# The next norm's sum of squares from block sums and a carried sum, at both junctions of a three-layer f32 kernel

## What is computed

```python
for i in range(2):                              # layers 0 (gated spatial unit) and 1 (latent attention)
    shift, scale, gate = split(silu(c) @ ada_w[i] + ada_b[i])
    h = rms_norm(x, pre_g[i]) * (1 + scale) + shift
    y = mixer_i(h)                              # ends with  ... @ w_out
    x = x + gate * rms_norm(y, post_g[i])
h = rmsnorm(x, norm_mix)                        # layer 2 begins so
z = h @ w_in
```

## Time and profile before

| | |
|---|---|
| median of 3 runs | 2478.34 us (2477.54 to 2480.36) |
| profiled execution | 2477.93 us, span 2476.1 us |
| PE busy | 2433.2 us (98%) |
| DVE busy | 1889.0 us (76%) |
| ACT busy | 1399.4 us (57%) |
| POOL busy | 442.0 us (18%) |

### The profile page before, as it was taken

The page is one execution under the profiler, slowest core; times in us unless marked ns, Lnnn a source line. Parts: engine busy times, 40 slices in busy tenths (PEclk is TensorE's granted clock), DMA queues, the critical chain, the costliest instruction groups (busy, mean ns, idle before and its releaser), DMA issues.

```text
span 2476.1 us, 31108 instructions
## 1 busy us (share of the span) xinstructions
PE 2433.2 (98%) x11597; PEld 2018.7 (82%) x11597; DVE 1889.0 (76%) x2295; ACT 1399.4 (57%) x1934; POOL 442.0 (18%) x298
## 2 busy tenths in 40 slices
PE   6999999999999999998999999999999999999999
PEld 5888888888887989887888888888888888888887
DVE  7899798977777787866655555557988878788884
ACT  6655765444447555555566676755655545555553
POOL 0264563111020000110000000043111021111111
PEclk9999999999999999999999999999999999999999
DMA  9999677978784877754555556455465555646454
GB/s 364 321 341 349 237 256 273 336 283 290 271 313 149 246 212 220 233 208 149 167 173 163 177 153 183 157 187 187 155 236 170 204 187 191 217 170 221 170 203 154
DMA packets 370999, 549.47 MB, mean 222 GB/s; under 512 B 31405, under 2 KB 158129, under 8 KB 370225
## 3 DMA queue, kind: packets, MB, share of 16 engines
q1 hardware_dynamic: 368688, 539.54, 64.6%
q10 hardware_dynamic: 1824, 6.04, 0.7%
q0 software_dynamic: 352, 2.11, 0.2%
HBM read 545.53 MB, written 2.11 MB: 221 GB/s over the span
## 4 chain that ended last, share of the span: by engine, by line
PE 88%; DVE 8%; ACT 2%; issue 1%; DMA 1%; SPq 0%; POOL 0%; DVEq 0%; ACTq 0%; POOLq 0%
PE ps L2393 48%; PE ps L2398 24%; DVE lo L1305 3%; PE ps L2423 2%; PE ps L2419 2%; PE ps L2420 2%; DVE ps L1330 1%; PE ps L2379 1%; PE ps L2378 1%; PE ps L2380 1%; DVE lo L1282 1%; DMA raw<-in_sgu_w_in 1%; PE ps L3007 1%; PE ps L2655 1%; ACT hi L630 1%
## 5 line engine op out<-in xcount | busy, mean ns | idle before, releaser
L1305 DVE TENSOR_TENSOR lo<-raw,hi 128x1024 fp32r<-128x1024 f32 x550 | 706.9, 1304 | 350.8 <-ACT hi L630 350.2
L630 ACT ACTIVATE hi<-raw 128x1024 fp32r<-128x1024 f32 x550 | 571.3, 1051 | 431.3 <-PE ps L2398 352.7
L2393 PE MATMUL ps<-hi,a_hi 128*128 128x512 f32 (+1 forms) x2016 | 798.6, 396 | 2.1 <-issue 0.9
L2393 PE MATMUL ps<-hi,a_lo 128*128 128x512 f32 (+1 forms) x2016 | 785.6, 390 | 0.0
L2398 PE MATMUL ps<-lo,a_hi 128*128 128x512 f32 (+1 forms) x2016 | 539.0, 389 | 1.5 <-DVE lo L1305 1.5
L616 ACT ACTIVATE hi<-raw 128x1024 fp32r<-128x1024 f32 x339 | 358.2, 1060 | 292.7 <-PE ps L2398 255.2
L1282 DVE TENSOR_TENSOR lo<-raw,hi 128x1024 fp32r<-128x1024 f32 x339 | 424.4, 1272 | 107.2 <-ACT hi L616 105.0
L2393 PEld LDWEIGHTS ps<-hi,a_hi 128*128 128x128 f32 x2016 | 378.7, 188 | 85.1 <-issue 5.3
L2398 PEld LDWEIGHTS ps<-lo,a_hi 128*128 128x128 f32 x2016 | 378.4, 188 | 81.1 <-DVE lo L1305 1.9
L2393 PEld LDWEIGHTS ps<-hi,a_lo 128*128 128x128 f32 x2016 | 378.9, 188 | 74.4
L2393 PE MATMUL ps<-hi,b_hi 128*128 128x512 f32 x880 | 347.4, 395 | 0.6 <-ACT y L1015 0.3
(11 more groups left out here) (351 smaller groups left out, 2436.6 us busy)
## 6 DMA issues: line engine op xcount, KB each, us to landing
raw<-in_sgu_w_in SPq DMA_DIRECT2D x88, 1024.0 KB
raw<-in_ada_w SPq DMA_DIRECT2D x64, 1024.0 KB
raw<-in_w_up SPq DMA_DIRECT2D x64, 1024.0 KB
raw<-in_w_down SPq DMA_DIRECT2D x64, 1024.0 KB
raw<-in_w_in SPq DMA_DIRECT2D x42, 1024.0 KB
raw<-in_ada_w SPq DMA_DIRECT2D x64, 512.0 KB
raw<-in_sgu_w_out SPq DMA_DIRECT2D x32, 1024.0 KB
raw<-in_w_in SPq DMA_DIRECT2D x128, 256.0 KB
```

The source lines that it names most:

```text
L630: nc.scalar.activation(hi[:, q % CHUNKS, 0:width], raw[:, r % RAWS, q % 2 * CW:q % 2 * CW + width], ACT.Copy).then_inc(hi_ready, 1)
L1305: nc.vector.tensor_tensor(lo[:, q % CHUNKS, 0:width], raw[:, r % RAWS, q % 2 * CW:q % 2 * CW + width], hi[:, q % CHUNKS, 0:width].bitcast( ...
L2393: nc.tensor.matmul(ps[:, 2 * s + t, 0:width], x[:, k0 + j, t * P:(t + 1) * P], hi[:, c, w], start=begins, stop=False)
```

## The change

The squares of the updated x go. In their place, for each block and tile, ScalarE squares the gated block (`act_gated_square`, sum into gx) and VectorE multiplies 2x by the gated block (`dve_crossed`, sum into gx); for blocks 0 to 2 both stand ahead of the junction. VectorE then makes the next var from a carried xsq (`dve_tile_next`). xsq begins as the opening norm's sum plus D * EPS. The results that nothing else reads (gated_parts, crossed_parts) go to bf16 views of v. All orders in the junctions are rewritten; at the first, TensorE's pair 0 comes ahead of the last chunk of tile 1, and of 12 + 10 passes of `unread` 6 remain (3 matmuls for 11). The diff, cut:

```diff
-def act_x_square(act, n, t, b, updated):
...
+def act_gated_square(act, t, b):
+
+    nc.scalar.activation(gated_parts[:, 2 * b + t, :], y[:, t, b * NB:(b + 1) * NB], ACT.Square,
+                         accum_out=gx[:, t, 0, b:b + 1]).then_inc(gated_sq, 1)
+
+def act_block_gated(act, layer, b):
+
+    act.wait_ge(y_gated, 6 * layer + 2 * b + 2)
+    if layer:
+        act.wait_ge(gated_sq, 8)
+    for t in range(T):
+        act_gated_square(act, t, b)
...
     act_tile_square(act, n, 0, 1)
     act_tile_root(act, n, 0)
+    act.wait_ge(acc_free, n.acc.base + 4)
+    act_gated_square(act, 0, 3)
+    act_tile_root(act, n, 0)
     act_steps(act, n, 1)
-    for b in range(4):
-        act_x_square(act, n, 0, b, b + 1)
+    act.wait_ge(scales, GROUPS + 1)
+    act_pair(act, n, 0, *PAIRS[0], 1)
     act.wait_ge(chunk_used, n.chunk.base + 2 + CHUNKS)
     act_tile_square(act, n, 1, 1)
+    act_tile_root(act, n, 1)
+    act_pair(act, n, 1, *PAIRS[1], 1)
+    act.wait_ge(acc_free, n.acc.base + 6)
+    act_gated_square(act, 1, 3)
     n.acc.base += 2
-    act_tile_root(act, n, 0)
     act_steps(act, n, 1)
+    act_pair(act, n, 2, *PAIRS[2], 1, rounds_only=True)
     act_tile_root(act, n, 1)
-    act.wait_ge(scales, GROUPS + 1)
-    act_pair(act, n, 0, *PAIRS[0], 1)
-    act_pair(act, n, 1, *PAIRS[1], 1)
-    act_x_square(act, n, 1, 0, 5)
-    act_steps(act, n, 1)
-    act_x_square(act, n, 1, 1, 6)
-    act_pair(act, n, 2, *PAIRS[2], 1, rounds_only=True)
     act_pair(act, n, 3, *PAIRS[3], 1, rounds_only=True)
-    act_x_square(act, n, 1, 2, 7)
-    act_x_square(act, n, 1, 3, 8)
-    act_steps(act, n, 1)
-    act_tile_root(act, n, 1)
+    act_steps(act, n, 2)
...
+    act.wait_ge(acc_free, n.acc.base + 5)
+    act_gated_square(act, 0, 3)
+    act_tile_root(act, n, 0)
     act_steps(act, n, 1)
-    for b in range(4):
-        act_x_square(act, n, 0, b, 8 + b + 1)
+    pairs = lambda *which: [act_pair(act, n, i, *TILE_PAIRS[i], None) for i in which]
+    pairs(0)
     act.wait_ge(chunk_used, n.chunk.base + 2 + CHUNKS)
     act_tile_square(act, n, 1, banks)
+    act_tile_root(act, n, 1)
+    pairs(1)
+    act.wait_ge(acc_free, n.acc.base + 6)
+    act_gated_square(act, 1, 3)
     n.acc.base += 2
-    act_tile_root(act, n, 0)
     act_steps(act, n, 1)
-    act_tile_root(act, n, 1)
-    pairs = lambda *which: [act_pair(act, n, i, *TILE_PAIRS[i], None) for i in which]
-    pairs(0, 1)
-    act_steps(act, n, 1)
-    act_x_square(act, n, 1, 0, 8 + 5)
-    act_x_square(act, n, 1, 1, 8 + 6)
     pairs(2, 3)
-    act_x_square(act, n, 1, 2, 8 + 7)
-    act_x_square(act, n, 1, 3, 8 + 8)
-    act_steps(act, n, 1)
     act_tile_root(act, n, 1)
     pairs(4, 5)
+    act_steps(act, n, 2)
...
+def dve_tile_rstd(dve, n, t, to=rstd):
+    nc.vector.reciprocal(to[:, t:t + 1], sd[:, t:t + 1]).then_inc(n_rstd, 1)
...
+def dve_crossed(dve, t, b):
+
+    at = slice(b * NB, (b + 1) * NB)
+    nc.vector.scalar_tensor_tensor(out=crossed_parts[:, 2 * b + t, :], in0=x[:, t, at], scalar=2.0, in1=y[:, t, at],
+                                   op0=ALU.mult, op1=ALU.mult, accum_out=gx[:, t, 1, b:b + 1]).then_inc(x_crossed, 1)
+
+def dve_block_crossed(dve, layer, b):
+
+    dve.wait_ge(y_gated, 6 * layer + 2 * b + 2)
+    for t in range(T):
+        dve_crossed(dve, t, b)
+
+def dve_tile_next(dve, n, layer, t):
+
+    one = slice(t, t + 1)
+    dve.wait_ge(x_crossed, 8 * layer + 7 + t)
+    dve.wait_ge(gated_sq, 8 * layer + 7 + t)
+    then(dve, n, nc.vector.tensor_reduce(gsum[:, t, :], gx[:, t, :, :], AX, ALU.add))
+    then(dve, n, nc.vector.scalar_tensor_tensor(out=cross[:, one], in0=gsum[:, t, 0:1], scalar=rgate[:, one], in1=gsum[:, t, 1:2],
+                                                op0=ALU.mult, op1=ALU.add))
+    then(dve, n, nc.vector.scalar_tensor_tensor(out=xsq[:, one], in0=cross[:, one], scalar=rgate[:, one], in1=xsq[:, one],
+                                                op0=ALU.mult, op1=ALU.add))
+    nc.vector.tensor_scalar(var[:, one], xsq[:, one], D * EPS, 1.0 / D, ALU.max, ALU.mult).then_inc(n_var, 1)
...
+    nc.vector.scalar_tensor_tensor(out=x[:, t, at], in0=y[:, t, at], scalar=rgate[:, t:t + 1], in1=x[:, t, at],
...
-def dve_x_normal(dve, t, b):
-
+def dve_x_normal(dve, t, b, updated):
+
+    dve.wait_ge(x_updated, updated)
...
+        if b:
+            dve_block_crossed(dve, 0, b - 1)
+        else:
+            then(dve, n, nc.vector.tensor_scalar(xsq[:, :], ss[:, :], D * EPS, None, ALU.add))
...
+    dve_block_crossed(dve, 0, 2)
...
+    dve_tile_rstd(dve, n, 0, rgate)
+    dve.wait_ge(acc_free, n.acc.base + 4)
+    dve_crossed(dve, 0, 3)
+    dve_tile_next(dve, n, 0, 0)
+    dve_x_update(dve, 0, 0)
+    dve_x_update(dve, 0, 1)
     dve_tile_rstd(dve, n, 0)
-    dve.wait_ge(y_gated, 6)
-    for b in range(4):
-        if b == 3:
-            dve.wait_ge(acc_free, n.acc.base + 4)
-        dve_x_update(dve, 0, b)
+    dve_x_normal(dve, 0, 0, 1)
+    dve_x_normal(dve, 0, 1, 2)
     dve_steps(dve, n, 1)
-    n.sq.base += 4
-    dve.wait_ge(n_ss, n.sq.base)
-    dve_tile_ss(dve, n, 0, xss)
+    dve_pair(dve, n, 0, *PAIRS[0], 1)
     n.bsq.base += 1
     dve.wait_ge(block_sq, 2 + n.bsq.base)
-    dve_tile_rstd(dve, n, 0)
-    for b in range(2):
-        dve_x_normal(dve, 0, b)
     dve_tile_ss(dve, n, 1, bss)
     dve_tile_gated(dve, 0, 1, 1, 2)
-    dve_tile_rstd(dve, n, 1)
-    dve_x_update(dve, 1, 0)
-    dve_pair(dve, n, 0, *PAIRS[0], 1)
-    dve_x_update(dve, 1, 1)
+    dve_tile_rstd(dve, n, 1, rgate)
+    dve.wait_ge(acc_free, n.acc.base + 6)
+    dve_crossed(dve, 1, 3)
     dve_modulated(dve, n, 2, *PAIRS[2], 1, 1)
     dve_pair(dve, n, 1, *PAIRS[1], 1)
+    dve_tile_next(dve, n, 0, 1)
     dve_modulated(dve, n, 3, *PAIRS[3], 1, 1)
-    dve_steps(dve, n, 1)
-    dve_x_update(dve, 1, 2)
-    dve.wait_ge(acc_free, n.acc.base + 6)
-    dve_x_update(dve, 1, 3)
+    dve_x_update(dve, 1, 0)
+    dve_tile_rstd(dve, n, 1)
     dve_pair(dve, n, 2, *PAIRS[2], 1)
-    dve_steps(dve, n, 1)
+    dve_x_update(dve, 1, 1)
+    dve_x_normal(dve, 1, 0, 3)
     dve_pair(dve, n, 3, *PAIRS[3], 1)
+    dve_x_normal(dve, 1, 1, 4)
     n.kept.base += 16
     n.acc.base += 2
     dve_steps(dve, n, 1)
-    n.sq.base += 4
-    dve.wait_ge(n_ss, n.sq.base)
-    dve_tile_ss(dve, n, 1, xss)
-    dve_tile_rstd(dve, n, 1)
-    dve_x_normal(dve, *PIECES[2])
-    dve_x_normal(dve, *PIECES[3])
+    dve_x_update(dve, 0, 2)
+    dve_steps(dve, n, 2)
+    dve_x_update(dve, 1, 2)
+    dve_x_update(dve, 0, 3)
+    dve_x_update(dve, 1, 3)
...
-    dve_steps(dve, n, 8)
+    dve_steps(dve, n, 4)
+    dve_block_crossed(dve, 1, 0)
+    dve_block_crossed(dve, 1, 1)
+    dve_steps(dve, n, 4)
+    dve_block_crossed(dve, 1, 2)
...
+    dve_tile_rstd(dve, n, 0, rgate)
+    dve.wait_ge(acc_free, n.acc.base + 5)
+    dve_crossed(dve, 0, 3)
+    dve_tile_next(dve, n, 1, 0)
+    dve_x_update(dve, 0, 0)
+    dve_x_update(dve, 0, 1)
     dve_tile_rstd(dve, n, 0)
-    dve.wait_ge(y_gated, 12)
-    for b in range(4):
-        if b == 3:
-            dve.wait_ge(acc_free, n.acc.base + 5)
-        dve_x_update(dve, 0, b)
-    dve_steps(dve, n, 1)
-    n.sq.base += 4
-    dve.wait_ge(n_ss, n.sq.base)
-    dve_tile_ss(dve, n, 0, xss)
+    dve_x_normal(dve, 0, 0, 9)
+    dve_x_normal(dve, 0, 1, 10)
+    dve_x_update(dve, 0, 2)
+    dve_x_update(dve, 0, 3)
+    dve_x_normal(dve, 0, 2, 11)
+    pairs = lambda *which: [dve_pair(dve, n, i, *TILE_PAIRS[i], None) for i in which]
+    pairs(0)
+    dve_x_normal(dve, 0, 3, 12)
     n.bsq.base += 1
     dve.wait_ge(block_sq, 2 + n.bsq.base)
-    dve_tile_rstd(dve, n, 0)
-    normal = lambda t, *blocks: [dve_x_normal(dve, t, b) for b in blocks]
-    pairs = lambda *which: [dve_pair(dve, n, i, *TILE_PAIRS[i], None) for i in which]
-    normal(0, 0, 1)
     dve_tile_ss(dve, n, 1, bss)
-    normal(0, 2, 3)
+    dve_steps(dve, n, 1)
+    pairs(1)
     dve_tile_gated(dve, 1, 1, banks, 1)
-    dve_tile_rstd(dve, n, 1)
+    dve_tile_rstd(dve, n, 1, rgate)
+    dve.wait_ge(acc_free, n.acc.base + 6)
+    dve_crossed(dve, 1, 3)
+    pairs(2, 3)
+    dve_tile_next(dve, n, 1, 1)
+    dve_steps(dve, n, 1)
     dve_x_update(dve, 1, 0)
     dve_x_update(dve, 1, 1)
-    pairs(0, 1)
+    dve_tile_rstd(dve, n, 1)
+    n.acc.base += 2
+    pairs(4, 5)
+    dve_x_normal(dve, 1, 0, 13)
+    dve_x_normal(dve, 1, 1, 14)
     dve_x_update(dve, 1, 2)
-    dve.wait_ge(acc_free, n.acc.base + 6)
     dve_x_update(dve, 1, 3)
     dve_steps(dve, n, 1)
-    pairs(2, 3)
-    n.acc.base += 2
-    n.sq.base += 4
-    dve.wait_ge(n_ss, n.sq.base)
-    dve_tile_ss(dve, n, 1, xss)
-    dve_tile_rstd(dve, n, 1)
-    normal(1, 0, 1)
-    dve_steps(dve, n, 1)
-    pairs(4, 5)
-    normal(1, 2, 3)
+    dve_x_normal(dve, 1, 2, 15)
+    dve_x_normal(dve, 1, 3, 16)
     dve_steps(dve, n, 1)
...
+    pe_by_tiles(pe, n, A, 1, range(8, 16, 2), ends=True, tells=True, before={(1, 0): columns, (1, 3): lambda: pair(0)})
+    n.acc.base += 2
     pe.wait_ge(acc_free, n.acc.at())
-    unread(0, 6)
```

(4 more changed lines are left out.)

23 lines of the change are left out of this document (12 added, 11 removed).

## The result

Against the kernel before on the same chip, medians of eight runs each: 2486.28 us (2483.82 to 2490.55) for 2480.61 us (2477.54 to 2481.77), ratio 1.0025, 95% interval 1.0015 to 1.0035. The change costs **5.7 us**; +5.6 was forecast. As a time the forecast was 2483.5 us, 2.8 under the measured one: 2.7 of them because it was added to one execution of before (2477.93 us), whose eight runs have their median at 2480.61. The profiled execution took 2485.41 us, 7.5 more than that of before.

A forecast was written before the change was run, and what follows sets the result against it. VectorE's queue was taken as the resource; queues 0.3 and 3.0, clock 2.2 and sum writing 0.1 gave +5.6 us on the profiled 2477.93 us: 2483.5 us, range 2478.5 to 2488.

The forecast's parts named there:

- (a): Chain to the first normalised block at each junction: 2.1 us earlier at the first, 1.85 us at the second.
- (b): VectorE's added work per junction: two cross products (1.33 us) and two more small operations per tile (0.76), 2.1 us.
- the 0.1 us that the forecast added for writing the sum: VectorE's cross products writing a sum on the side: +0.1 us in all, a price no row shows.
- (c): Cross products and gated squares of blocks 0 to 2, moved ahead of the junctions: costed at nothing.
- (d): First junction's queues: product starts earlier, TensorE then stands 3.8 us for the second chunk's late lo; +0.3 us.
- (e): Second junction's queues: product starts 1.4 us earlier, then ScalarE's pair 2 and late lo's delay it; +3.0 us.
- (f): Granted clock falls in two new stretches: 1.0 us at the first junction, 1.2 at the second, +2.2 us.
- A: Rival: no further fall of the clock, the queue's +3.4 us stands alone, 2481.3 us; chance 0.30.
- B: Rival: late lo's are not what TensorE waits for, head start kept at both junctions, 2475.0 us; chance 0.10.
- C: Rival: a VectorE cross product is much slower than an update, +3.8 us on the forecast, 2487.3 us; chance 0.10.

The follow-up runs named there:

- the run with the clock held: Changed kernel plus unread products in TensorE's new stands at both junctions, each shorter than its stand; ratio 1.0015 to the kernel before, junctions 49.38 and 40.72 us.
- the lo's early: Changed kernel with VectorE's order alone rewritten, lo's of chunks 2 to 4 ahead of later updates at both junctions; 2480.83 us for 2480.38 before, ratio 1.0001.

## Why the prediction came out right

*(a) The normalised block earlier:* right. 763.66 less the offset for 765.72, 2.06 us for 2.1; at the second 1124.10 for 1125.87, 1.77 for 1.85.

*(b) VectorE's new work:* right in the sum. A cross product in the junctions is 0.61 from start to start and not 0.66, so the 0.1 us that the forecast added for writing the sum was nothing; behind a small operation with three inputs the next comes 0.25 us later and not 0.19. *(c) hidden ahead:* right; the lo part at 757.33 is where 756.10 and the offset put it, and the time between the junctions is the same to 0.01 us. More was hidden than was laid out: the two cross products of block 0 took 1.60 and 1.77 us, not 0.66 (last section).

*(d), (e) the queues:* right, +0.48 for +0.3 and +2.99 for +3.0 us (the run with the clock held). The lay-out of the queue named the late lo's, ScalarE's pair 2 and the two long stands in place and length. The 0.2 us missing at the first lie in its start: tile 1's sum comes at 766.79, the offset taken off, and not at 766.6, and all behind keeps about that distance (the lo 773.86 for 773.7; with the clock held the fifth pair's remainder 0.17 late). The shorter cross product and the longer small operations cancel there.

*(f) the clock:* that it falls in both stretches was right; its two prices were mis-sized, in opposite directions: 0.37 us for 1.0 at the first junction, below its bounds of 0.6 to 1.4; 2.38 us for 1.2 at the second, the upper bound of 0.9 to 2.4. At the first I took off too little of what hides behind VectorE, though my own lay-out had VectorE as the later one at the fifth pair. At the second I took one chunk at the slow rate, "one chunk" for no better reason than that the fourth chunk came next; the clock was back only 5.3 us after work resumed, nearly two chunks and the pairs between them later, where TensorE and not VectorE was the later one. In other executions of the same instructions the parts were up to 0.7 and down to 1.6 us, so no single price could have been right.

*Rivals.* A (no further fall) is out by the rows of the clock. B (the head start is kept) is out by the stands of 3.74 and 2.03 us, but its condition was the right one: with the lo's early the first junction takes 47.53 us, 1.4 under before. C (a slow cross product) is out by the 0.61 us in the junctions. Its remark that the updates contradict a halved rate goes further than the rows do (last section).

*The total.* By terms 0.85 + 5.37 = 6.2 us in the profiled pair, 5.7 between medians, +5.6 forecast; the errors of the terms (0.5 too much at the first junction, 1.1 too little at the second) partly cancel, so the total is better than its working: that it came within 0.1 us is luck. The same instructions also differ between executions by when the clock falls: the second junction new by itself took 42.33 us. Counted from the junction's start its clock was at 0.5 from 27.3 to 34.1 us, in the changed kernel from 29.1 to 35.9, while the fourth chunk starts at 30.6 us in both: in the one the low stretch ends 3.5 us into the work, in the other 5.3. That the moment of the fall makes the difference fits these rows, but no run varied it alone. In the old order of this junction the moment made none: the low stretch was from 14.1 to 20.9 us in the kernel before, from 15.4 to 22.2 and from 16.1 to 22.9 in the two runs with only the first junction new, and the spans were 37.73, 37.74 and 37.72.

## What to carry to other kernels

A shorter chain is worth nothing if the queue that carries it is already the resource and the rewritten order puts what the other engine waits for behind what nobody needs yet: lay out the queue, and place each remainder by the start of its use. Before an order is judged, judge it at its best: the same instructions lose 6.2 us over the two junctions in one order and win 2.5 in another. A fall of the clock cost nothing here in an order where VectorE was the later one behind it, and up to 2.4 us, nearly half of the 5.3 us that TensorE worked in it, where none was, so price it at the next point where the engines meet, and as a range.

## What was not expected of the hardware

A VectorE operation that also writes a sum shows as two instructions, and the second adds nothing. Timeline of VectorE, changed kernel:

```profile
758.33 0.69 DVE L1508 SCALAR_TENSOR_TENSOR v<-x,y 128x512 f32<-128x512 f32 x1
758.94 0.08 DVE L1508 DVE_READ_ACCUMULATOR v<-x,y 128x1 f32 x1
758.94 0.69 DVE L1508 SCALAR_TENSOR_TENSOR v<-x,y 128x512 f32<-128x512 f32 x1
```

The next operation starts with the read, 0.61 us after the first; ScalarE's read takes 0.19. That there are two is what the Trainium skill says, "VectorE: DVE Perf Modes", section "Two Vector instructions with no wait between them", and the trace agrees. The Trainium skill, "Vector Engine (DVE) Microarchitecture Reference", section "7. Points that are easy to get wrong", says that this shape halves its rate with two SBUF sources that are not bf16, as no port is left for the accumulator. What the trace shows is that the sum itself costs no rate: with f32 sources the operation with a sum is as fast as the update without one, 0.61 for 0.66 us. Half of what rate that section means, and whether bf16 sources would be faster than both, no run here shows.

Not every cross product is that fast. Those of block 0, ahead of the first junction (timeline of VectorE; the third line is from that of GpSimd):

```profile
721.10 1.60 DVE L1508 SCALAR_TENSOR_TENSOR v<-x,y 128x512 f32<-128x512 f32 x1
722.64 1.77 DVE L1508 SCALAR_TENSOR_TENSOR v<-x,y 128x512 f32<-128x512 f32 x1
720.86 3.00 POOL L2271 TENSOR_TENSOR y<-y,stage 128x512 f32<-128x512 f32 x2 [13.75 <-ACT stage L654]
```

They take 3.2 us together for 1.2, while GpSimd multiplies y of both tiles, and it was so in every run with these sums at the first junction (the longest took 1.77 us each time). That GpSimd slows them is likely but not shown, as no run moved them apart. TensorE lost nothing by it.

An unread f32 product of 128 columns is two rows and 0.23 us of TensorE (14 of them: 28 rows, 3.29 us).
